# Logits of the next cached block ahead of this block's products with values, from step 14 of a 68-step attention loop

## What is computed

```python
k_full = cache_k[page_table].reshape(DB, 16, 256, H, Dh)
gate = einsum('bthd,bjhd->bhtj', q, mean(k_full, axis=2))
sel = top_k(gate, 3)                       # three of sixteen blocks of 256 keys
logits = concat(q . k of the selected blocks, causal(q . k of the new tokens))
out = softmax(logits * scale) . values
```

## Time and profile before

| | us |
|---|---|
| Three runs | 1440.32, 1445.76, 1450.32 |
| Their median | 1445.76 |
| The profiled execution | 1439.12 |
| Its span, first to last instruction | 1437.3 |
| Busy in the span: PE, PEld | 1265.2, 1132.7 |
| Busy in the span: DVE, POOL, ACT | 634.7, 450.9, 414.5 |

### The profile page before, as it was taken

One profiled execution on the slowest core, in us unless ns is written; L12 is line 12 of the kernel. 1 busy time (PEld: TensorE's weight loads), 2 busy tenths in 40 slices (PEclk: granted clock), 3 DMA queues, 4 the chain that ended last, 5 costly groups with the idle time before them and its releaser, 6 DMA issues. The chain is left out here.

```text
span 1437.3 us, 33488 instructions
## 1 busy us (share of the span) xinstructions
PE 1265.2 (88%) x14346; PEld 1132.7 (79%) x14346; DVE 634.7 (44%) x1113; ACT 414.5 (29%) x829; POOL 450.9 (31%) x309
## 2 busy tenths in 40 slices
PE   4999997887888988888652999999999999999995
PEld 3998994755666665666332999998999999999995
DVE  6368884362545555344259211133454554450003
ACT  4142322122332323222232222233333433341110
POOL 5244442010101110111002333353555555555430
PEclk9999998898999999999865999999999999999998
DMA  4222208667787787856810222322122222322221
GB/s 192 79 102 74 74 32 304 228 235 286 268 303 265 293 320 298 307 214 243 334 74 0 88 84 78 104 74 98 60 89 74 88 87 76 104 86 81 82 72 66
DMA packets 57254, 216.32 MB, mean 150 GB/s; under 512 B 6609, under 2 KB 6994, under 8 KB 56338
## 3 DMA queue, kind: packets, MB, share of 16 engines
q1 hardware_dynamic: 57106, 214.17, 41.2%
HBM read 207.78 MB, written 6.37 MB: 149 GB/s over the span
## 5 line engine op out<-in xcount | busy, mean ns | idle before, releaser
L580 PE MATMUL ps<-buffer_at 128*128 128x288 f32 (+2 forms) x5760 | 775.0, 297 | 35.9 <-ACTq L1247 30.9
L580 PEld LDWEIGHTS ps<-buffer_at 128*128 128x128 f32 x5760 | 771.1, 190 | 40.7 <-POOL buffer_at L1326 36.8
L1326 POOL TENSOR_TENSOR buffer_at<-buffer_at 128x1024 fp32r<-128x1024 f32 (+1 forms) x118 | 332.4, 2819 | 295.9 <-ACT buffer_at L1063 295.3
L1063 ACT ACTIVATE buffer_at<-buffer_at 128x1024 fp32r<-128x1024 f32 (+1 forms) x118 | 128.9, 1095 | 250.8 <-PE ps L580 134.0
L1388 POOL TENSOR_TENSOR buffer_at<-buffer_at 128x256 f32<-128x256 f32 x45 | 40.0, 918 | 397.2 <-DVE buffer_at L1623 397.2
L892 PE MATMUL ps<-buffer_at 128*32 128x256 f32 x1024 | 78.9, 428 | 25.4 <-DMA buffer_at<-in_kvcache 24.7
L1961 DVE TENSOR_TENSOR buffer_at<-ps,buffer_at 128x512 f32<-128x512 f32 x44 | 30.4, 691 | 126.3 <-PE ps L580 126.2
L923 PE MATMUL ps<-buffer_at 128*32 128x128 f32 x2048 | 75.3, 288 | 12.0 <-ACT buffer_at L1186 7.5
L1297 ACT ACTIVATE buffer_at<-buffer_at 128x592 f32<-128x592 f32 x44 | 38.9, 883 | 162.5 <-DVE buffer_at L1963 159.2
L1722 DVE TENSOR_REDUCE buffer_at<-ps 128x1 f32<-128x256 f32 (+1 forms) x68 | 28.0, 412 | 109.7 <-PE ps L892 108.6
L923 PEld LDWEIGHTS ps<-buffer_at 128*32 128x32 f32 x2048 | 55.5, 114 | 21.3 <-ACT buffer_at L1186 10.2
(11 more groups left out here) (217 smaller groups left out, 1455.1 us busy)
## 6 DMA issues: line engine op xcount, KB each, us to landing
buffer_at<-in_kvcache SPq DMA_DIRECT2D x256, 512.0 KB, 5.0
buffer_at<-in_w_up SPq DMA_DIRECT2D x44, 512.0 KB, 3.5
buffer_at<-in_w_in SPq DMA_DIRECT2D x42, 512.0 KB, 3.5
buffer_at<-in_w_down SPq DMA_DIRECT2D x16, 704.0 KB, 3.9
buffer_at<-in_w_br SPq DMA_DIRECT2D x8, 512.0 KB, 3.5
buffer_at<-in_w_o SPq DMA_DIRECT2D x8, 512.0 KB, 3.5
buffer_at<-in_xin SPq DMA_DIRECT2D x4, 576.0 KB, 6.9
buffer_at<-in_xin SPq DMA_DIRECT2D x1, 2304.0 KB, 12.1
```

The source lines that it names most:

```text
L580: ins = e.matmul(out, lhs, rhs[:, cols], start=(start and i == 0), stop=(stop and i == 2))
L1063: e.activation(hi[:, :, :], raw, ACT.Copy).then_inc(w_hi, 1)
L1326: e.tensor_tensor(lo[:, :, :], raw, hi[:, :, :], ALU.subtract).then_inc(w_lo, 1)
```

## The change

For steps 14 to 66 (`TWO < i < STEPS - 1`) the matrix engine issues the logits of block i + 1 straight after part 0 and the products with values of block i after part 1. The scalar engine takes the exponentials of block i + 1 where it copied out the product of block i, and copies that out where it took the exponentials. The vector engine takes the lowest logit of block i + 1 before the prompt's piece of part 1 instead of after it. No instruction is added or removed; the other steps keep their order.

```diff
+def logits_first(i):
+    return TWO < i < STEPS - 1
...
             for i in range(STEPS):
                 turn_step(i)
                 chunk_stage(stage_at(i, 0))
+                if logits_first(i):
+                    qk_step(i + 1)
+                    side_work(i, 1)
+                    pv_step(i)
+                    chunk_stage(stage_at(i, 2))
+                    side_work(i, 3)
+                    continue
                 pv_step(i)
                 side_work(i, 1)
                 if i + 1 < STEPS:
...
                 chunk_copies(stage_at(i, 0))
-                o_out(i)
+                if logits_first(i):
+                    exp_step(i + 1)
+                else:
+                    o_out(i)
                 attention(2 * i)
                 if i >= A_STEPS:
                     chunk_copies(stage_at(i, 1))
-                if i + 1 < STEPS:
+                if logits_first(i):
+                    o_out(i)
+                elif i + 1 < STEPS:
                     exp_step(i + 1)
...
                 att_second(2 * i - 1)
+                if logits_first(i):
+                    low_step(i + 1)
                 if i >= A_STEPS:
                     chunk_out(stage_at(i, 1))
                 if p >= 0 and j == 11 and turn_part(i) == 1:
                     o_rows(p)
                 att_first(2 * i)
-                if i + 1 < STEPS:
+                if i + 1 < STEPS and not logits_first(i):
                     low_step(i + 1)
```

## The result

The changed kernel took 1460.78 us (median of 18 runs, 1443.26 to 1473.12), the kernel before 1445.27 (18 runs, 1439.68 to 1451.85); the medians differ by 1.07%. The ratio of 1.0081 (95% interval 1.0053 to 1.0109, some 12 us) leaves out six runs of the changed kernel that lie more than 1.5% above its fastest and count as a slower state. The forecast was 1452.3 / 1445.8 = 1.0045, + 6.5 us. So sign and range came out, and the class (within 1%) by the first ratio, while e1 stands just outside; the size was about half.

What follows compares the result with a forecast made beforehand. The matrix engine was taken to set the pace almost everywhere, the cache stream just behind. Paced stretches + 5.1, bare end + 4.8 and gains - 3.4 gave + 6.5 us on 1445.8: 1452.3 us, range 1436 to 1470.

Steps and rivals of the forecast that it cites:

- What bounds the kernel, and what the change does to a step: Whole loop: matrix engine sets the pace, cache stream just behind; its work is unchanged, each fill loses 3.6 us of slack.
- The loop, 2T = L + q + a + p: Step time T from freed-buffer-to-landed-fill time L plus logits q, side piece a and values p: at least 6.32 us.
- I take L = 9.84: Time from freed buffer to landed fill, taken from the fill for step 38: 9.84 us.
- a = 0.8: Side piece between logits and values in a step: 0.8 us, from 0.36 to 1.9 in the steps looked at.
- Stretches that now run below 6.32 are stretched to it; the others keep their pace: Steps 19 to 25, 30 to 33 and 43 to 48 slow to 6.32 us each: together + 5.1 us.
- The bare end, + 4.8: Last steps without side piece, fill-bound: 6.41 us a step, + 4.0, and + 0.8 after the last fill.
- the clock: Rival: every wait for a fill drops the clock to 1.2 GHz; + 24 at most, 1476; chance 0.06.
- + 0.8 after the last fill: Bare end: values of step 66 (1.93) stand where 1.13 us of waiting stood, + 0.8.
- The gains, - 3.4: Earlier exponentials save six times 0.4 = 2.4 before d products from step 48; two waits for turned exponentials give 1.0.
- DVE and ACT at nothing: New order on vector and scalar engines priced at nothing, with bounds of + 4.8 and - 4.8 us.
- What would show it: Signs: logits waiting 0.2 to 2 us, steps of 6.2 to 6.5; wrong if transposes wait much unlike 15.7 us.
- the ring is slower: Rival, same 20 steps: transfers keep the end's 11.5 us, step 7.15 us; + 23, 1469; chance 0.18.

Runs made afterwards that it cites:

- e1: The changed kernel unaltered, run again for a second profile, against the kernel before: ratio 1.0106 (1.0081 to 1.0132), + 15.3 us.
- g1: Old order, but from fill 14 on a transfer fetches 128 of its 1024 columns, against the kernel before: ratio 0.9869 (0.98 to 0.9938).
- g2: Changed order, with from fill 14 on 128 of 1024 columns fetched per transfer, against the kernel before: ratio 0.9816 (0.9751 to 0.9881).
- f1: Old order, SP reads a fill's four page numbers ahead of its wait for the buffer, against the kernel before: ratio 0.9989 (0.9952 to 1.0026).
- e2: Changed order in steps 14 to 47 alone, against the kernel before: ratio 1.0062 (1.0038 to 1.0086), + 8.9 us.
- e4: Changed order in the bare steps 60 to 66 alone, against the kernel before: ratio 1.0028 (0.9996 to 1.0060), + 4.0 us.
- e3: Changed order in steps 48 to 59 alone, against the kernel before: ratio 1.0011 (0.9984 to 1.0039), + 1.6 us.
- f: f1 and f2 together: page numbers read ahead of SP's wait, in the old and the changed order; ratios 0.9989 and 0.998 against the kernel before.
- j: f2 with the old order in the bare end (changed order in steps 14 to 59 only), against the kernel before: 0.9961 (0.9935 to 0.9987), 1436.32 us.
- f2: Changed order, SP reads a fill's four page numbers ahead of its wait for the buffer, against the kernel before: ratio 0.998 (0.9944 to 1.0015).
- h_split_old: Old order, page numbers read ahead, each fill split into separately released key and value transfers, against the kernel before: 0.988 (0.9843 to 0.9917), 1425.18 us.

## Why the prediction was right in kind and short in size

**What bounds the kernel, and what the change does to a step: right.** Between steps 15 and 48 and in the bare end the logits wait for the cache, in steps 49 to 60 never; the DMA engines are less busy than before, and g1 against g2 show no cost of the pieces in the changed order. One reading was wrong: of the waits "in steps 13 and 14, which still use two buffers" the second, 5.1 us, isn't the ring's. Fill 13 is the first into the third buffer, and SP issues it only when the store of the recurrence's state has landed. SP's wait for that store in the kernel before, read from 300 to 345 us:

```profile
SPq L489 <- DMA out_wkvs<-buffer_at: 8.2, 1, 8.2
```

The matrix engine waits for this fill in every kernel that was profiled here (9.1 us in f1), so it takes no part in the change.

**The loop, 2T = L + q + a + p: right as a formula.** In the chain above, L is 402.18 - 390.53 = 11.65 and 416.28 - 405.40 = 10.88, the stretch from logits to the end of the values 3.22 and 2.66; the four add up to the 28.41 us. They must, but both logits waited for their fill, so it is L that sets the pace there. Bare end: values of step 62 end at 720.56, logits 65 start at 730.70 (L 10.14), values 64 end at 734.34 (3.64), logits 67 start at 743.48 (9.14), values 66 end at 747.12 (3.64): 26.56 us for 4 steps, 6.64 each.

**"I take L = 9.84": the first term that was too small.** It came from one fill, and from a short one. Worked out in the same way, the 48 fills of steps 18 to 67 have a median L of 10.64 in the kernel before, and those of steps 21 to 25 a mean of 10.5. In e1 the median is 10.05 and the mean of steps 21 to 25 is 10.63. So waiting did thin the traffic out over the whole (DMA share 81% from 94%, median landing 4.9 us against 5.2), but from a higher start, and in those short steps it took nothing off. By the formula 10.63 gives 6.71 for them; measured 6.76.

**"a = 0.8": the second.** The side piece between the logits and the values now waits itself, since the logits ahead of it have come late and everything on DVE behind them too. In steps 44 to 48 of e1 it is 3.53 us on average from the start of the logits to the end of the values, where I had 2.8. With the L of those steps, 9.5 to 10.4, that is 6.66 us a step; measured 6.96.

**"Stretches that now run below 6.32 are stretched to it; the others keep their pace": the step that failed in kind.** A stretch is not a step. Fills hold the short steps (the shortest of before are 5.0 us) and leave the long ones as they are, so a stretch's mean ends above the pace of the ring, and a stretch with a mean over 6.32 isn't safe: in e1 logits waited 1.0 to 1.4 us in each of steps 16, 29, 38 and 39, none of them in a named stretch. For steps 14 to 47 I had + 5.1 and - 1.0 for the values' two waits; e2 measured + 8.9 (5.5 to 12.4). In waits the miss is larger: from 336 to 592 us the logits waited 17.0 us more for the cache (27.9 in place of 10.9), and part of it came back in other waits, 5.0 from the transposes and 3.3 from the values.

**The bare end, + 4.8: right in size by e4, + 4.0 (- 0.6 to + 8.7); + 5.9 in the profile from logits 61 to 67; in part by luck.** "About half and half, so I take the middle, 6.41" was the weak step: all logits from step 62 on took 1.93 or 1.94 us, so the formula's 6.85 for the lower clock was the one to take, with an L of 9.1 to 11.4. The rival *the clock* came true here, at 0.62, but not in the stretch that was looked at in the middle of the loop: at 384 to 425 us the clock is 1.00 in spite of waits of 1.7 to 2.3 us in three of the steps. The Trainium skill, "TensorE: Matmul & The Clock Gate", section "HAM oscillation — how this bites in real kernels", describes a loop that starts cold in every turn because it waits for a transfer in each; the bare end agrees, the middle of the loop doesn't. The + 0.8 after the last fill wasn't there: from logits 67 to the end of the loop it is 6.23 us before and 6.35 after. So + 4.8 is near because one term was too small and another stood for nothing.

**The gains, - 3.4: mechanism right, size not shown.** The d products wait 0.56 us in the steps that I looked at instead of 0.90, 3.5 in all instead of 4.5, so the six times 0.4 were more than double the 1.0 that came. By e3 the part is + 1.6 (- 2.3 to + 5.6), with - 2.4 just outside, while its profile is 1.9 us shorter there: a gain is neither shown nor excluded.

**DVE and ACT at nothing: no cost was seen, and there may be a gain.** From logits 14 to 60 g2 is 5.3 us shorter than g1. Of these 3.4 were counted as gains, and the other 2 lie well within the - 4.8 that bounded this term. But the place is another: from the turn of step 14 to that of step 48, where 1.0 was counted, it is 4.5 us (223.8 against 228.3), and steps 25 to 30 above belong to it. What gains there stays open. No logits were found waiting for the gate sum.

**What would show it.** DMA share, and the two waits that go, came as said. Logits waited in all bare steps, but in the named stretches in 7 of 14, by 1.4 to 3.1 us, and not in most by 0.2 to 2. Steps of 6.2 to 6.5 us didn't come (6.7 to 7.0). Transposes waiting much less than 15.7 us, a sign of being wrong, did (10.7). "SP's wait for values shorter" was wrong: from 384 to 425 us it went from 10.0 to 22.7 us. SP's own work for a fill is the same; where the matrix engine's step is longer, SP waits longer. So the rival *the ring is slower*, which was to decide from L = 10.6 on, was half true: 10.05 in the median and 10.63 in steps 21 to 25, in place of 9.84 or 11.5.

## What to carry to other kernels

When a consumer is moved earlier past the step that frees its own ring's buffer, write the loop from freed buffer to landed data to next freed buffer, and set it against each single step, not against the mean of a stretch. Take L from many fills, not from one. Reading the page numbers ahead was enough for the 1% to go, as far as f can tell. One event that frees two things at the later of their last uses is worth taking apart: with early page numbers, and keys and values fetched and released separately, the kernel went from 1443.96 to 1421.83 us, though the old order gained as much by it. And a part of the loop without other work (here the last eight steps) lost time with the changed order in every profile; keeping the old order there (j) shortened that part by 8.5 us, while a shorter time than f2's isn't shown. A fourth buffer, the plainest test of the ring, was not tried.

## What the runs showed that I had not expected

Issuing a fill's four transfers back to back made the issue 2 us shorter and the landing of the last one longer, so L gained only 0.9 us (10.05 to 9.18), as much as the first issue came earlier.

Smaller transfers carry less at the same share of busy time. In the bare end of the kernel before, with 512 KB a transfer (stretch, busy, clock, DMA share, GB/s):

```profile
692.00:699.00 7.00, 3.62 (x83) 2.35 (x83) 2.22 (x8) 1.58 (x7) 0.00 (x0) 1.00 0.98 366
```

and in that of h_split_old, with 256 KB:

```profile
699.00:706.00 7.00, 4.56 (x50) 2.35 (x50) 0.85 (x2) 1.36 (x6) 0.00 (x0) 0.50 0.98 327
```

The share is 98% in both, the rate 366 and 327 GB/s. Over a longer stretch, 345 to 540 us, it is the same: 296 GB/s at 80% before, 295 at 89% in h_split_old. The Trainium skill, "DMA: Bandwidth & Descriptors", section "Rules for kernel authors", wants large transfers for the highest rate; these two rows agree. The split won in spite of it, as can be where buffers more than bytes hold the loop.
